# Moving the logits, masks and exponentials of the first softmax pair of heads into the dense unit and the top-value rounds ahead of them

## The reference, cut to what matters

```python
proj = x @ w_in + b_in      # [q_a|k_a|v_a|g_a|q_b|k_b|v_b|g_b|q_idx|k_idx|w_idx|r_a|r_b]
# branch A: stick-breaking attention on q_a, k_a, v_a (8 heads of 64)
# branch B: sparse attention (8 heads of 64, one shared key and value head)
index_score = einsum('bth,bths->bts', w_idx, relu(q_idx . k_idx))   # -inf where not admissible
_, sel = lax.top_k(index_score, n_select)                           # 128 prompt, 80 sample
logits = q_b . k_b[sel] * ATT_SCALE + rel_bias[t5_bucket(...)]
p = softmax(logits); y_b = p @ v_b[sel]
merged = sigmoid(r_a) * (y_a*silu(g_a) @ w_pa) + sigmoid(r_b) * (y_b*silu(g_b) @ w_pb)
x = layer_norm(ALPHA * x + merged @ w_out)
```

## Time and profile before

| | |
|---|---|
| median of three executions | 1026.46 us |
| the profiled execution, its own time | 1024.89 us |
| its span (first to last instruction) | 1023.1 us |
| mean granted TensorE clock over the span | 0.997 |
| PE busy | 990.9 us (97%) |
| DVE busy | 618.0 us (60%) |
| ACT busy | 485.4 us (47%) |
| POOL busy | 524.0 us (51%) |

### The profile page before, as it was taken

One profiled execution on the slowest core, in us unless ns is written; L12 is line 12 of the kernel. 1 busy time (PEld: TensorE's weight loads), 2 busy tenths in 40 slices (PEclk: granted clock), 3 DMA queues, 4 the chain that ended last, 5 costly groups with the idle time before them and its releaser, 6 DMA issues.

```text
span 1023.1 us, 18374 instructions
## 1 busy us (share of the span) xinstructions
PE 990.9 (97%) x7336; PEld 908.9 (89%) x7336; DVE 618.0 (60%) x1217; ACT 485.4 (47%) x836; POOL 524.0 (51%) x470
## 2 busy tenths in 40 slices
PE   6999999999999999999999999999999999999997
PEld 5889997778899999998888899777888999999985
DVE  7479998879953300450864899978898321100147
ACT  6564326668957222222235633466788542222320
POOL 2436556536556545657424365555465565545550
PEclk9999999999999999999999999999999999999999
DMA  7512542111112425223343134301111222252222
GB/s 238 188 58 79 168 148 88 43 37 44 47 42 68 139 82 187 79 84 127 95 157 110 42 95 129 129 1 43 43 42 43 84 67 83 90 183 83 89 88 93
DMA packets 70120, 95.43 MB, mean 93 GB/s; under 512 B 4482, under 2 KB 61300, under 8 KB 69396
## 3 DMA queue, kind: packets, MB, share of 16 engines
q1 hardware_dynamic: 66084, 82.69, 24.9%
q0 software_dynamic: 3776, 11.50, 3.2%
q10 hardware_dynamic: 176, 0.07, 0.0%
HBM read 81.04 MB, written 14.79 MB: 94 GB/s over the span
## 4 chain that ended last, share of the span: by engine, by line
PE 78%; DVE 15%; ACT 2%; issue 2%; POOL 2%; DMA 0%; DVEq 0%; ACTq 0%; POOLq 0%
PE ps L567 36%; PE ps L874 10%; PE ps L929 9%; PE ps L789 4%; DVE attn L1531 4%; DVE attn L1504 3%; DVE top L1528 3%; PE ps L591 3%; PE ps L810 2%; PE ps L768 2%; PE ps L849 2%; PE ps L828 2%; PE ps L750 2%; PE ps L615 1%; PE ps L737 1%
## 5 line engine op out<-in xcount | busy, mean ns | idle before, releaser
L1778 POOL TENSOR_TENSOR w_lo<-raw,w_hi 128x512 fp32r<-128x512 f32 x115 | 156.0, 1357 | 362.1 <-ACT w_hi L980 361.9
L567 PE MATMUL ps<-xT_hi,w_hi 128*128 128x288 f32 x864 | 256.2, 296 | 0.3 <-POOL w_lo L1779 0.3
L567 PE MATMUL ps<-xT_hi,w_lo 128*128 128x288 f32 x864 | 254.5, 295 | 0.0
L567 PE MATMUL ps<-xT_lo,w_hi 128*128 128x288 f32 x864 | 254.4, 294 | 0.0
L980 ACT ACTIVATE w_hi<-raw 128x1024 fp32r<-128x1024 f32 (+1 forms) x116 | 121.3, 1046 | 108.1 <-PE ps L567 71.2
L567 PEld LDWEIGHTS ps<-xT_hi,w_hi 128*128 128x128 f32 x864 | 162.1, 188 | 1.7 <-POOL w_lo L1779 0.9
L567 PEld LDWEIGHTS ps<-xT_lo,w_hi 128*128 128x128 f32 x864 | 162.1, 188 | 0.0
L567 PEld LDWEIGHTS ps<-xT_hi,w_lo 128*128 128x128 f32 x864 | 162.0, 188 | 0.0
L1779 POOL TENSOR_TENSOR w_lo<-raw,w_hi 128x512 fp32r<-128x512 f32 x115 | 157.2, 1367 | 0.0
L1731 DVE TENSOR_TENSOR qy<-qy,ps 128x576 f32<-128x576 f32 x32 | 24.1, 754 | 204.5 <-PE ps L567 204.5
L1089 ACT ACTIVATE qy<-ps,bias 128x576 f32<-128x576 f32 x33 | 24.5, 742 | 127.0 <-PE ps L567 126.9
(11 more groups left out here) (235 smaller groups left out, 2334.5 us busy)
## 6 DMA issues: line engine op xcount, KB each, us to landing
raw<-in_w_in SPq DMA_DIRECT2D x44, 1024.0 KB, 5.1
raw<-in_w_out SPq DMA_DIRECT2D x8, 1024.0 KB, 5.0
x_kept<-x_nat SPq DMA_DIRECT2D x2, 2560.0 KB, 10.3
x_nat<-x_kept SPq DMA_DIRECT2D x2, 2560.0 KB, 12.4
raw<-in_w_proj_a SPq DMA_DIRECT2D x8, 512.0 KB, 3.6
raw<-in_w_proj_b SPq DMA_DIRECT2D x8, 512.0 KB, 4.6
x_nat<-in_x_prompt SPq DMA_DIRECT2D x4, 512.0 KB, 5.2
out<-stage POOLq DMA_DIRECT2D x8, 256.0 KB, 5.0
```

The costliest lines, as they stand in the source:

```text
L567: last = mm(out, a, b[:, HALF * half:HALF * (half + 1)], start=(k == 0 and i == 0), stop=(k == n - 1 and i == 2))
L1778: g.tensor_tensor(lo[:, 0:half, :], src[:, 0:half, :], hi[:, 0:half, :].bitcast(f32), ALU.subtract)
```

## The change

PE issues `logits(0)` between the two halves of unit 17, with the waits that it needs there (position bias, low parts of keys and queries, the evacuation of unit 16, whose banks it takes). DVE runs `masked_logits(0)` and `(1)` inside the rounds of the sample tile, after round index 5 in the first layer and 3 in the second. ACT loads the table and runs `exp_row(0)` and `(1)` ahead of the evacuation of unit 17. In the loop, round 0 of PE has only `logits(1)`, and round 1 has `logits(2)` at its start and `logits(3)` after the `qa_group` of p = 2. DVE's order after the sample mask becomes `qa_half(0)`, `normalise(0)`, `masked_logits(2)`, `(3)`, `normalise(1)`, then `masked_logits(4)`. POOL's and SP's programs are as they were. No instruction is added or dropped.

```diff
-                def product(g, stationary, moving, rows_out):
+                def product(g, stationary, moving, rows_out, between=None):
...
+                        if half == 0 and between:
+                            between()
                     last.then_inc(s_grp, 1)
...
+                def first_logits():
+
+                    pe.wait_ge(s_bn, 16)
+                    pe.wait_ge(s_kblo, L * 2 + 2)
+                    pe.wait_ge(s_qblo, L * 4 + 4)
+                    pe.wait_ge(s_ev, L * N_EV + act_evacs(N_QA - 1))
+                    logits(0)
...
-                    product(GROUP[u], st, mv, HD + NH if kind == "KI" else 128)
+                    product(GROUP[u], st, mv, HD + NH if kind == "KI" else 128, first_logits if u == N_QA - 1 else None)
...
                 for r in range(NBP // 2 + 1):
-                    if r < NBP // 2:
-                        logits(2 * r)
-                        logits(2 * r + 1)
+                    if r == NBP // 2:
+                        stick_z(0)
                     else:
-                        stick_z(0)
+                        if r:
+                            logits(2 * r)
+                        if r != 1:
+                            logits(2 * r + 1)
...
                         qa_group(*QA_GROUPS[p])
+                        if p == 2:
+                            logits(3)
...
                 for u in range(7, N_QA):
+                    if u == N_QA - 1:
+                        act.preload_act_table_set("natural_log_exp_and_others")
+                        exp_row(0)
+                        exp_row(1)
                     evacuate(u)
...
-                act.preload_act_table_set("natural_log_exp_and_others")
-
...
-                            if p < NBP:
+                            if 0 < p < NBP:
                                 exp_row(2 * p + hh)
...
                         dve.wait_ge(s_top, L * N_TOP + n_top)
+                        if kind == "s" and r == (5, 3)[L]:
+                            masked_logits(0)
+                            masked_logits(1)
...
-                for r in range(NBP // 2):
-                    if 2 * r - 1 in QA_HALF_AT:
+                qa_half(QA_HALF_AT[1])
+                normalise(0)
+                masked_logits(2)
+                masked_logits(3)
+                normalise(1)
+                for r in range(1, NBP // 2):
+                    if r > 1 and 2 * r - 1 in QA_HALF_AT:
                         qa_half(QA_HALF_AT[2 * r - 1])
                     masked_logits(4 * r)
                     masked_logits(4 * r + 1)
```

More of the change, by code:

```diff
@@ L568, in product, with logits @@
                                           start=(k == 0 and i == 0), stop=(k == n - 1 and i == 2))
+                        if half == 0 and between:
+                            between()
                     last.then_inc(s_grp, 1)
+                def logits(p):
+                    ti, m = divmod(p, PAIRS)
+                    tt, t0, n, k0, nk, _, _ = tile_of(*BT_ORDER[ti])
+                    if p >= 2:
+                        pe.wait_ge(s_rm, L * N_B + 2 * p - 2)
+                    for i, (q, k) in enumerate(((q_hi, kb_hi), (q_hi, kb_lo), (q_lo, kb_hi))):
+                        for hh in range(2):
+                            half = slice(64 * hh, 64 * hh + 64)
+                            last = mm(ps[0:n, (2 * p + hh) % 4, 0:nk], q[half, m, t0:t0 + n], k[half, k0:k0 + nk],
+                                      start=(i == 0), stop=(i == 2))
+                            if i == 2:
+                                last.then_inc(s_lg, 1)
+                def first_logits():
[4 more added lines that the diff above has]
+                    logits(0)
                 def dense(u):
@@ L723, in _ @@
                 to_token_major(N_TR - 1)
[L725 to L740, removed]
                 def transpose_probs(s):
@@ L1212, in token_major, with exp_row @@
                     act_f(dst, src, ACT.Copy).then_inc(s_trev, 1)
+                def exp_row(s):
+                    ti, h = divmod(s, NH)
+                    _, _, n, _, nk, _, _ = tile_of(*BT_ORDER[ti])
+                    act.wait_ge(s_rm, L * N_B + s + 1)
+                    if s >= P_SLOTS:
+                        act.wait_ge(s_ri, L * NBP + (s - P_SLOTS) // 2 + 1)
+                    c = slice(s % P_SLOTS, s % P_SLOTS + 1)
+                    act_f(prob[0:n, s % P_SLOTS, 0:nk], prob[0:n, s % P_SLOTS, 0:nk], ACT.Exp, bias=row_min[0:n, c],
+                          scale=-1.0, accum_out=row_sum[0:n, c]).then_inc(s_ex, 1)
                 for u in range(7, N_QA):
+                    if u == N_QA - 1:
+                        act.preload_act_table_set("natural_log_exp_and_others")
+                        exp_row(0)
+                        exp_row(1)
                     evacuate(u)
@@ L1224, in _ @@
                 token_major(N_TR - 1)
[L1227 to L1235, removed]
                 def move_probs(s):
@@ L1516, in _, with masked_logits @@
                             done.then_inc(s_kblo, 1)
+                def masked_logits(s):
+                    ti, h = divmod(s, NH)
+                    _, _, n, _, nk, _, _ = tile_of(*BT_ORDER[ti])
+                    dve.wait_ge(s_lg, L * N_B + s + 1)
+                    if s >= P_SLOTS:
+                        dve.wait_ge(s_pt, L * N_B + s - P_SLOTS + 1)
+                    dve.wait_ge(s_mb, L * N_B + s + 1)
+                    c = s % P_SLOTS
+                    v.tensor_tensor_reduce(out=prob[0:n, c, 0:nk], in0=ps[0:n, s % 4, 0:nk],
+                                           in1=mask_bias[0:n, s % 2, 0:nk], scale=1.0, scalar=-TAKEN,
+                                           op0=ALU.add, op1=ALU.min,
+                                           accum_out=row_min[0:n, c:c + 1]).then_inc(s_rm, 1)
                 dve.wait_ge(s_acc, L * NH * N_IDX + NH * N_IDX)
@@ L1536, in _ @@
                 assert n_top == N_TOP
[L1539 to L1552, removed]
                 def normalise(p):
```

## The result

The changed kernel takes 1030.82 us (median of 8 runs, 1029.21 to 1033.4) beside 1026.8 us for the kernel before on the same chip (8 runs, 1025.31 to 1028.03): a ratio of 1.0043 with the interval 1.0031 to 1.0055. So it is slower by 4.4 us by the ratio (4.0 by the medians), where 2.4 us were forecast (1028.9), and just outside the range of 1026.3 to 1030.6. The direction was right, the size was not: the result lies near the 1031.3 of rival C, the clock.

The account below looks back on a forecast made before the run. PE, busy 97% of the span, bounds the kernel, with DVE setting its waits; order, break and port add 1.7 us in layer 0 and 0.75 in layer 1, +2.4 on 1026.46 gives 1028.9 us, range 1026.3 to 1030.6.

Parts of the forecast that it names:

- rival C: Clock falls behind PE's 2.6 us wait in each layer: +2.4 us more, 1031.3 us; chance 0.06.
- The landmark: Start of `masked_logits(4)` on DVE, which the end follows; forecast 1.03 us later in layer 0, 0.09 in layer 1.
- The distance: From the end of the second `qa_group` on PE to `masked_logits(4)` on DVE: 4.69 us, before 3.66 and 4.60.
- The order term: DVE's new instruction order delays `masked_logits(4)` by 1.03 us in layer 0 and 0.09 us in layer 1.
- The break: `logits(0)` interrupting PE's dense matmuls ahead of `qa_half(0)`: about 0.3 us per layer, bounds 0 and 0.4.
- the port: POOL's DMA instruction holding off DVE's multiplications in `normalise(0)`: 0.35 us per layer, bounds 0 and 0.78.
- the lower bound: No loss of DVE's multiplications beside POOL's DMA, from a trace row at 628.30 us: 0 per layer.
- PE's new wait: One PE wait of about 2.6 us ahead of pair 1's transposes, replacing the 0.8 us wait for `qa_half(0)`.
- A: Rival: port free and break cheap, so only DVE's order counts: +1.3 us, 1027.8 us; chance 0.30.
- B: Rival: DVE's lead removes PE's waits: -2.2 us, 1024.3 us, needing 2.9 us from group's end to `masked_logits(4)`; chance 0.12.
- D: Rival: early logits arrive late and DVE waits within its sample rounds; 1028.9 us again, counted with the forecast's 0.52.

Follow-up runs that it names:

- x1: The changed kernel with 20 transposes of the identity added on PE ahead of the transposes of pair 1, into unread PSUM: ratio 1.0018 to the kernel before.
- the repeat: The changed kernel, unaltered, run again on one chip beside its versions with 20 and 10 filler transposes; the kernel before took 1026.64 us there.
- x4: The kernel before with only PE's `logits(0)` moved between the halves of unit 17: ratio 1.0011.
- x2: The changed kernel with DVE's old order after the sample mask: `masked_logits(2)`, `(3)`, `normalise(0)`, `(1)`, `qa_half(0)`: ratio 1.0018 to the kernel before.
- y3: The kernel before with DVE's new order alone after the sample mask, PE, ACT and POOL as before: ratio 1.0008.
- x3: The changed kernel with DVE's order `normalise(0)`, `masked_logits(2)`, `(3)`, `qa_half(0)`, `normalise(1)`: ratio 1.0004 to the kernel before.
- y4: The changed kernel with POOL's bias rows 2, 3 ahead of unit 19's low part, DVE's order `masked_logits(2)`, `(3)`, `normalise(0)`, `qa_half(0)`, `normalise(1)`: 1024.42 us, ratio 0.9984.

## Why the prediction missed: right steps, and the one that failed

**The landmark and the order: right.** `qa_half(0)` is DVE's first instruction behind the sample mask, with 2.67 and 0.77 us of idle time before it (forecast: about 2, and little). `exp_row(3)` is waited for, 0.98 us (0.8). The distance is 5.02 us (4.69): 0.14 us of the difference is the start of `qa_half(0)` behind its group, which I had taken at once (159.87 to 160.00, and 0.44 for 0.43), 0.19 the multiplications beside the DMA. The order term was 1.03 and 0.09, without the DMA; it measures 1.17 and 0.24.

**The order alone, priced whole: right.** Forecast 1.7 and 0.75 for order, break and port; measured 1.81 and 0.82 in x1, where no fall is in the way. The break costs 0.4 per layer (0.3), the port 0.19 (0.35); they were off in opposite directions, so the closeness of the sum is in part luck. The upper bound of 0.78 for the port is not borne out. Nor was the row that stood for the lower bound evidence: the DVE operation that ended at 628.58 had begun at 627.33, ahead of the DMA instruction at 628.30, so it shows nothing of one that finds such an instruction running.

**PE's new wait: right.** Forecast one wait of about 2.6 us ahead of the transposes of pair 1; it is 2.46 to 2.5 in both layers. The chain goes as forecast, through `qa_half(0)`, `masked_logits(4)`, the exponential and the move (chain of waits of the changed kernel, 150 to 172 us, beside the earlier trace rows):

```profile
160.00 0.52 DVE attn L1598
...
164.97 0.60 DVE attn L1539
165.62 0.81 ACT attn L1231 x2
166.43 0.48 ACT attn L1258
```

**The clock: the step that failed.** The forecast priced the new wait by its length only: its sum has no term for the clock, which it held as rival C with a chance of 0.06, though it named a falling clock as a sign of being wrong. The runs show it as about half of the loss. Over 197 single runs of the ten kernels, one slope holds, each kernel with a level of its own: 0.72 us for each 0.001 of mean granted clock, scatter 0.45 us (the kernel before: 1024 us at 0.999, 1028.6 at 0.993; the changed one: 1029.2 to 1029.9 at 0.995, 1033 at 0.990). The runs of the changed kernel have 0.9928 and 0.9930, those of the kernel before 0.9961 to 0.9963, so (0.0031 to 0.0035) x 720 = 2.2 to 2.5 us. With the 2.6 us of x1's profile that gives 4.8 to 5.1 us; measured 4.4 and, in the repeat, 5.3. (At equal clock the same fit puts the changed kernel 2.5 us above the kernel before, and x1_warm20 2.2.) That the wait has a part in it is shown, not argued: work put into the wait and nowhere else gave back 2.6 us, and 3.5 in the repeat, by the ratios. One fall costs 1.4 to 1.7 us of PE's busy time, the longer one of the changed kernel's second layer 3.0; the earlier trace rows, from which I had worked out 1.2 for C, had the size nearly right. What was wrong was the chance. I had let the full clock behind waits of up to 0.8 us speak for a wait three times as long.

The Trainium skill ("TensorE: Matmul & The Clock Gate", section "HAM oscillation — how this bites in real kernels") describes gaps in which TensorE waits for data and after which the next tile starts at the low level. The trace agrees with it in three of the four profiled layers of the changed kernel, as in the first: 2.46 us of wait, then 0.57 over the 4 us from 168; in the fourth the clock stayed at 1.00 behind the same wait. The section deserved more weight than I gave it.

**What stays open.** Which waits bring a fall is not settled. In the profiles it came behind waits of 2.5, 2.4, 2.2, 2.0, 1.5 and 1.2 us, behind several short ones in x4's second layer and one of 0.7 us in x2, and in the changed kernel's repeat in the first layer and not in the second; with 10 transposes in the wait, in one layer of four; with 20, in none of four. It did not come behind 2.0 us in y3's first layer nor behind 1.6 and 1.3 us in x3. In the kernel before the profile has none in the softmax, but its single runs range from 0.993 to 0.999. So a long wait makes a fall likely, not certain.

**POOL's queue: missed, and harmless by luck.** I let POOL's low part shift by 1.1 us and looked only at its user. Behind it in the same program stand the bias rows 2 and 3; they end at 158.45 + 1.32 = 159.77 in the changed kernel, and only because `qa_half(0)` holds DVE until 160.00 does nobody wait for them. In x4 and x2 somebody does. Removing that queue, with `qa_half(0)` one place earlier than in x2, made the fastest version; the two were not tried apart.

**The rivals.** A (1.3 us) fell: the break and the port cost 0.6 per layer together. B (faster) asked for a distance of 2.9 us or less in the first layer: with the changed order it is 5.02, with y4's 2.31, and then the time does fall; with x3's 3.49 it does not. Its point of decision fits. D as good as did not occur: DVE waited 0.3 us in its rounds, 0.2 in the second layer.

## What to carry to other kernels

Price a new wait of PE twice: by its length, and by the fall of the clock behind it, which here cost as much again; filler matmuls in the wait show which of the two it is. In an engine's program, put the work that is ready ahead of the instruction that must wait. When a step moves, follow the delay through every engine's queue, to the instructions that stand behind the late one and not only to its user.

## What the runs showed of the hardware that was not expected

- Twenty transposes of 128x128 in a wait of 2.5 us kept PE at full clock in four layers of four, at 2.40 us for the twenty.
- DVE's multiplications are longer beside a DMA instruction of POOL, and by how much depends on how they meet. Two that started 0.36 us into a DMA instruction of 0.78 us took 1.07 us instead of 0.88 (the changed kernel, both layers). In y4, the two that took 2.23 us started in the first of two such instructions (159.01 to 160.47 us) and met a POOL operation of 0.69 us behind them; even if that held them whole, 2.23 - 0.88 - 0.69 = 0.66 us are left for the DMA instructions. No experiment moves these instructions alone. POOL's timeline there:

```profile
159.01 0.56 POOL L1848 DMA_DIRECT2D out<-attn  x1
159.57 0.90 POOL L1849 DMA_DIRECT2D out<-attn  x1
160.48 0.69 POOL L1870 TENSOR_TENSOR attn<-mask,bias_near 128x256 f32<-128x256 bf16 x1
```

- Six matmuls of 64 rows inside a dense run cost 0.4 us per layer over their own time, which only went to another place (13.42 to 13.81 us up to the group's end).
